# A hybrid decoder layer with 32 experts: the order of the expert tiles and of the weight loads is changed

## What is computed

```python
def hier_moe(h, rg_w, rg_b, re_w, re_b, w_gate, w_up, w_down):
    # top-1 of 4 expert groups, then top-2 of the 8 experts in it: 2 experts for each token
    ...
    def expert_block(args):
        xblk, e = args
        return (jax.nn.silu(xblk @ w_gate[e]) * (xblk @ w_up[e])) @ w_down[e]
    ...
    y = jnp.sum(yb[dest].reshape(T, TOP_K, D) * gate[..., None].astype(h.dtype), axis=1)
```

## Time and profile before

| | |
|---|---|
| median of 3 runs | 1059.0 us (1054.67 to 1060.1) |
| profiled execution | 1059.32 us, its span 1057.6 us |
| TensorE busy (PE) | 960.4 us, 91% |
| VectorE busy (DVE) | 659.9 us, 62% |
| ScalarE busy (ACT) | 459.9 us, 43% |
| moved by DMA | 264.97 MB, 251 GB/s over the span |

### The profile page before, as it was taken

The page is one execution under the profiler, slowest core; times in us unless marked ns, Lnnn a source line. Parts: engine busy times, 40 slices in busy tenths (PEclk is TensorE's granted clock), DMA queues, the critical chain, the costliest instruction groups (busy, mean ns, idle before and its releaser), DMA issues.

```text
span 1057.6 us, 12148 instructions
## 1 busy us (share of the span) xinstructions
PE 960.4 (91%) x4539; PEld 685.7 (65%) x4539; DVE 659.9 (62%) x752; ACT 459.9 (43%) x554; POOL 341.4 (32%) x245
## 2 busy tenths in 40 slices
PE   6999999999999998499999899989986898999981
PEld 5758888887878887375564464455423576888861
DVE  5468999788786677774420431232104587999975
ACT  6576446343662223254220321231104385777762
POOL 0276998932120000202231032022110343423234
PEclk9989999999999999599999999999999989999996
DMA  9520202020072324889799999999999999999774
GB/s 318 173 81 1 80 1 80 0 81 1 5 275 100 120 99 161 312 292 374 271 354 393 414 347 340 417 362 328 420 412 421 410 408 343 356 379 387 263 258 187
DMA packets 65294, 264.97 MB, mean 251 GB/s; under 512 B 10853, under 2 KB 29477, under 8 KB 40656
## 3 DMA queue, kind: packets, MB, share of 16 engines
q1 hardware_dynamic: 51792, 237.07, 57.4%
q0 software_dynamic: 10032, 18.60, 7.1%
q10 hardware_dynamic: 3408, 8.48, 2.1%
HBM read 249.44 MB, written 28.84 MB: 263 GB/s over the span
## 4 chain that ended last, share of the span: by engine, by line
PE 33%; DMA 19%; DVE 5%; ACT 2%; issue 1%; POOL 1%; SPq 0%; POOLq 0%; ACTq 0%; DVEq 0%
PE ps L2260 7%; DMA raw_b<-in_expert_w_down_dram 7%; PE ps L2233 6%; PE ps L2235 6%; PE ps L2234 6%; DMA raw_b<-in_expert_w_up_dram 5%; PE ps L2273 4%; DMA summed_rows<-ym,idx_g 3%; DMA raw<-in_expert_w_up_dram 2%; PE ps L2226 2%; DMA raw<-in_expert_w_down_dram 1%; DVE lo_a L1765 1%; DMA xg<-hf_rows,idx_g 1%; DVE sums L1857 1%; ACT hi_a L1203 1%
## 5 line engine op out<-in xcount | busy, mean ns | idle before, releaser
L2233 PE MATMUL ps<-hi_a,xm_hi 128*128 128x512 f32 x304 | 126.4, 416 | 20.6 <-DVE lo_b L1765 10.3
L824 POOL DMA_INDIRECT summed_rows<-ym,idx_g x25 | 60.8, 2431 | 215.5 <-DVE ym L1814 208.0
L2235 PE MATMUL ps<-hi_a,xm_lo 128*128 128x512 f32 x304 | 124.1, 408 | 0.0
L2260 PE MATMUL ps<-raw,xm 128*64 128x512 f32 x256 | 112.5, 594 | 4.7 <-DMA raw_b<-in_expert_w_up_dram 4.3
L1765 DVE TENSOR_TENSOR lo_a<-raw,hi_a 128x2048 fp32r<-128x2048 f32 x32 | 72.8, 2289 | 65.3 <-ACT hi_a L1203 65.3
L2260 PE MATMUL ps<-raw_b,xm 128*64 128x512 f32 x256 | 112.6, 595 | 0.7 <-DMA raw<-in_expert_w_up_dram 0.7
L1376 DVE SCALAR_TENSOR_TENSOR ps<-uT,pcol,ps 128x1024 f32<-128x1024 f32 (+1 forms) x87 | 96.5, 1109 | 2.4
L735 POOL TENSOR_TENSOR acc<-x,acc 128x1024 f32<-128x1024 f32 x30 | 85.6, 2854 | 31.1 <-ACT x L995 27.0
L1765 DVE TENSOR_TENSOR lo_b<-raw_b,hi_a 128x2048 fp32r<-128x2048 f32 x28 | 63.7, 2291 | 37.7 <-ACT hi_a L1203 37.6
L2233 PEld LDWEIGHTS ps<-hi_a,xm_hi 128*128 128x128 f32 x304 | 59.5, 196 | 39.9 <-DVE lo_b L1765 12.6
L809 POOL DMA_INDIRECT xg<-hf_rows,idx_g x27 | 32.0, 1185 | 160.1 <-PE ps L2226 136.5
(11 more groups left out here) (366 smaller groups left out, 2338.8 us busy)
## 6 DMA issues: line engine op xcount, KB each, us to landing
raw_b<-in_expert_w_gate_dram SPq DMA_DIRECT2D x32, 1024.0 KB, 12.4
raw_b<-in_expert_w_up_dram SPq DMA_DIRECT2D x32, 1024.0 KB, 14.3
raw<-in_expert_w_up_dram SPq DMA_DIRECT2D x32, 1024.0 KB, 14.2
raw<-in_expert_w_gate_dram SPq DMA_DIRECT2D x32, 1024.0 KB, 10.8
raw_b<-in_expert_w_down_dram SPq DMA_DIRECT2D x32, 1024.0 KB, 12.3
raw<-in_expert_w_down_dram SPq DMA_DIRECT2D x32, 1024.0 KB, 11.9
raw<-in_w_in_dram SPq DMA_DIRECT2D x8, 1024.0 KB, 7.1
xa<-in_x_dram SPq DMA_DIRECT2D x8, 512.0 KB, 8.8
```

The source lines that it names most:

```text
L824: return pool.indirect_dma_start(out=sum_dram, out_offset=bass.IndirectOffsetOnAxis(ap=at.bitcast(U32), axis=0), in_=src, in_offset=None, ...
L2233: pe.matmul(dst, x_hi, w_h, start=first, stop=False)
L2235: return pe.matmul(dst, x_lo, w_h, start=False, stop=stop)
L2260: last = pe.matmul(ps[r * BL:(r + 1) * BL, i // 2, :], xm[:, kk, r * BL:(r + 1) * BL], slot(n, i)[:, w], start=(kk == 0), stop=(kk == KC - 1))
```

## The change

Two things. First, `KINDS` is another string with the same counts of each kind. Before, it reads `SS PDEP PDEP PDEP PP` and 11 times S; after, `SSPSPDEPSPDEPDEPSPSSSSSSPSS`. The last two tiles are S in both; the third last is S before and P after. Second, `load_order` comes from a function that runs at build time. It goes through the pieces in the order in which TensorE uses them and gives each a nominal time, and it lets a nominal load queue take 2.9 us for each piece. Whenever that queue is free, it picks, of all pieces whose slot is free by then, the one with the earliest first use.

```diff
-    KINDS = "SS" + "PDEP" * 3 + "PP" + "S" * 11
+    KINDS = "SSPSPDEPSPDEPDEPSPSSSSSSPSS"
...
-        load_order = sorted(((n, i) for n in range(FIXED, NE) for i in range(6)),
-                            key=lambda p: (slot_free(p[0] - 2, p[1])[1], first_use(*p), p))
+        def planned_loads():
+
+            used = sorted(((after_piece(t, i), t, i) for t in range(NS) for i in range(6)))
+            wanted = [(n, i) for n in range(FIXED, NE) for i in range(6)]
+            landed = {(n, i): 0.0 for n in range(FIXED) for i in range(6)}
+            done, queue, plan = [0.0], 0.0, []
+            while wanted:
+                ready, end = len(done) <= len(used), 0.0
+                if ready:
+                    k, t, i = used[len(done) - 1]
+                    ready = all((n, i) in landed for n in tile_pos[t])
+                if ready:
+                    split = 0.0 if KINDS[t] == "P" else T_SPLIT
+                    end = max([done[-1]] + [landed[n, i] + split for n in tile_pos[t]])
+                    end += (T_PAIR if KINDS[t] == "P" else T_ONE) + (T_TURN if i == 3 else 0.0)
+                free = [p for p in wanted if slot_free(p[0] - 2, p[1])[1] < len(done)]
+                now = [p for p in free if done[slot_free(p[0] - 2, p[1])[1]] <= queue]
+                if now and (not ready or queue <= end):
+                    p = min(now, key=lambda p: (first_use(*p), p))
+                    wanted.remove(p)
+                    queue += T_LOAD
+                    landed[p] = queue + T_LAND
+                    plan.append(p)
+                elif ready:
+                    done.append(end)
+                else:
+                    queue = max(queue, min(done[slot_free(p[0] - 2, p[1])[1]] for p in free))
+            return plan
+
+        T_LOAD, T_LAND, T_SPLIT, T_ONE, T_PAIR, T_TURN = 2.9, 2.0, 4.3, 2.85, 3.25, 1.5
+        load_order = planned_loads()
```

## The result

The kernel after the change takes 1047.29 us (median of 7 runs, 1045.44 to 1051.27), the kernel before, beside it on the same chip, 1056.66 us. The ratio is 0.9914, with a 95% interval from 0.9889 to 0.9939: faster by 0.6 to 1.1%. The prediction said 1061, and that a change of more than 0.5% to the faster side had a chance of 0.28. The time is within its range (1044 to 1074), on the side that it thought less likely.

The account below looks back on a forecast made before the run. TensorE was busy 91%, with about 49 us lost between 510 and 891 us, where weight loads set the pace in the fullest stretch. Sum: 1059.3 - 9 + 10 = 1060.3, given as 1061 us; range 1044 to 1074.

Parts of the forecast that it names:

- the stage: From tile 1's first piece to the end of tile 24's down part; a gain of 9 us was forecast before that end.
- Step 1: Spreading the pairs in the tile order: 47 us lost against 49, so hardly anything gained by itself.
- The ledger: DMA against TensorE time per tile: a pair owes 10 us, D with E gives back 16, 11 absorbed per group.
- Step 2: Loads by need instead of slot release: 7.6 us less lost, from 47 to 39.4, rounded to 40.
- The upper bound: Load order: 7.6 us more absorbed in each of three losing groups, lost time falling from 47 to 24 us.
- The hold at place 29: Loads held some 16 us behind a wait for expert place 29's piece 0; no cost while the DMA queue is long.
- the plan's waits starve the DMA queue: Slower rival: 10 us lost at expert place 29, 1071 us; chance 0.14 together with the rival of held scatters.
- Step 3: After tile 24, now a pair: two scatters in sequence instead of one, +10 us, low +7, high +14.
- The rule on the port: DVE with two SBUF inputs contends with GpSimd reading SBUF, the second blocks; both scatters after tile 24 in danger.
- the order is worth what it could be: Faster rival: 24 us stay lost instead of 49, the end costs 8; 1042 to 1050 us; chance 0.28.
- the debt stays: Slower rival: nothing gained before tile 24 and the longer end is paid; 1068 us; chance 0.20.
- The signs: Tile 24's last scatter landing 20 to 22 us after its down projection; TensorE loss near 40 us; wrong if idle under 30.

Follow-up runs that it names:

- tiles_only: Kernel before with the new tile order and the old sort of the loads; 1062.35 us.
- single_and_down: Kernel before; at four places behind a pair, the single expert's gate and up pieces, then the pair's down pieces, go ahead of the later expert's; 1048.99 us.
- single_first: Kernel before; at four places behind a pair, only the single expert's four gate and up pieces go ahead of the later expert's; 1058.3 us.
- nominal_25: Kernel after with the planner's nominal time for a load at 2.5 instead of 2.9 us; 1039.34 us.
- squares_late: Kernel after with ScalarE's first square of the summed rows moved behind the last tile's down splits; 1047.81 us.

## Why the prediction was wrong in its direction

**The sum in parts.** In the profiled executions the stage was to give 9 us and gave 18.2, the tail was to cost 10 and cost 8.0, and 3.7 us came from ahead of both; against the median there is also the base, as the sum starts from an execution of 1059.3 us and the kernel before had a median of 1056.66.

**Step 1, the tile order: nearly right.** The ledger gave 47 us lost instead of 49. Measured by itself (tiles_only) the new tile order loses 36.3 us of idle time and some 15 us by the low clock, together 52 us in the stage. The 47 take 11 us as absorbed also in the first group, where the same paragraph had found 6; with 6 there the ledger gives 52. That spreading the pairs "brings hardly anything by itself" held under the old sort. What the ledger hadn't in it is that the two parts interact: under the plan the same tile order is worth 6 us of the stage, and the tail takes them back. Also, "each stall is followed by a time at the lower clock" isn't so in its own rows: 577.3 to 618.0 us has 8.0 us of idle time at PEclk 1.00. The sum of 10.2 us takes it as 0, rightly.

**Step 2, the load order: this step failed, in its size.** What moves was named, with places and rows. The upper bound, 23 us, held for the change: the stage was 20.3 us shorter than with the old sort in the same tiles (540.9 to 520.6). With 2.5 us it was 26.0 us shorter, beyond that bound. I took a third of it, 7.6 us, "being nearer to the measured margin than to the ideal one". The reason given, that the order "shifts need, it removes no transfer", is where it went wrong. No transfer is removed, but idle time of the queue is: pieces that TensorE needs sooner free their slots sooner, and SP's gaps shrink (single_and_down: 13.3, 14.6 and 15.0 us instead of 20.4, 22.4 and 23.6). The row of that gap was in front of me; I used it as proof that what is given back can't be stored, and took it for fixed. Also, I counted the D tiles' pieces only. The single_first run shows that these by themselves are worth nothing (1058.3 us), the next one that with the pairs' down pieces they are worth 8 us in the old tiles. In the new tiles no run takes the planned order apart like this.

**The hold at place 29: wrong in kind, right in the sum.** It was to last some 16 us and lasted 18.1. It was to cost nothing because issue to landing was 20.9 us. But that latency is the one among pairs; here, behind S tiles, the queue was short and ran dry (49 GB/s). The rival "the plan's waits starve the DMA queue" is thus seen, yet not its 10 us: the other order of the same loads costs as much. Nothing shows that the pair's stall of 5.3 us of idle and 3.5 us of low clock could be had for less by ordering.

**Step 3, the tail: right in kind, 2 to 4 us off.** +10 was forecast, +8.0 measured between the two profiled executions, and about 6 over all of them. The second scatter is issued 7.6 us after the first (8.9 forecast) and lands in 4.6 us (9.2 forecast, the median over all pairs. The last pair holds the smallest experts of its kind, and fewer loads are under way then; no run parts the two). That makes 12.3 us instead of 7.9, +4.3. Another 2.8 us come from ahead of it: the first scatter goes out 6.1 us after the down part instead of 3.3, since VectorE writes `ym` behind two splits of a last tile, and these begin with the end of the down part instead of 2.7 us ahead of it; their tile's pieces land late (ScalarE had waited 8.1 us for one of them, until 978.2 us). This wasn't in the sum. About 1 us of the 8.0 lies behind the last scatter. It landed 18.3 us after the down part, below the 20 to 22 that I gave as the sign.

**The rule on the port.** The prediction named the tail's two scatters as being in danger. The Trainium skill, page "SBUF — State Buffer", section "Who interferes with whom", says that a DVE instruction with two SBUF inputs contends with a GpSimd instruction that reads SBUF, and that the shared ports are an exclusive lock. In one direction the traces agree. While the scatter instruction of 861.50 us before lasted 10.01 us, DVE did this (start us, us, line, op):

```profile
861.12 2.29 DVE L1765 TENSOR_TENSOR lo_a<-raw,hi_a 128x2048 fp32r<-128x2048 f32 x1
863.32 4.50 DVE L1765 TENSOR_TENSOR lo_b<-raw_b,hi_b 128x2048 fp32r<-128x2048 f32 x2
867.73 2.30 DVE L1765 TENSOR_TENSOR lo_b<-raw_b,hi_a 128x2048 fp32r<-128x2048 f32 x1
```

A subtraction of two SBUF operands was already running when the scatter began, three more followed at once, and the scatter ended 1.49 us after the last of them. This is no exception. In the 14 profiled executions such a subtraction was running at the start of 116 scatters, and each of these ended 1.3 to 1.5 us after the end of a subtraction; the other 347 took 1.45 to 1.64 us. In the other direction the traces don't agree. The timelines of POOL and of DVE in the tail after the change:

```profile
990.55 1.45 POOL L853 DMA_INDIRECT summed_rows<-ym,idx_g  x1 [21.18 <-DVE ym L1843]
998.18 1.58 POOL L853 DMA_INDIRECT summed_rows<-ym,idx_h  x1 [6.19 <-DMA summed_rows<-ym,idx_g]
```

```profile
990.71 2.29 DVE L1794 TENSOR_TENSOR lo_a<-raw,hi_a 128x2048 fp32r<-128x2048 f32 x1 [0.45 <-ACT hi_a L1232]
```

The subtraction starts 0.16 us into the scatter instruction and runs 2.29 us; the scatter takes 1.45 us. All 1344 such subtractions of the 14 executions take 2.26 to 2.35 us, also those that begin while a scatter instruction runs (118 scatters had one). So a scatter that comes second waits, and a subtraction that comes second doesn't. Here the tail's two scatters had luck. In three of the six kernels with the pair at tile 24 the second one met a subtraction, took 3.4 to 3.5 us (nominal_25: 990.73 us, 3.36 us) and landed after 6.3 to 6.6 us instead of 4.6.

**The rivals.** The faster one, 0.28, was the right one: "the order is worth what it could be", 24 us lost and 1042 to 1050. Measured were 32 us lost (52 with the old sort in the same tiles) and 1047.3. I argued against it that the DMA share is full from 769.8 to 831.1 and that no order makes room there. That is true of the stretch and beside the point: there was room elsewhere, where the queue ran dry (before, at 515 and 612 us). What speaks for "the debt stays" fell with the run of the load order alone.

**The signs.** Idle time plus low clock was to be near 40 us; it was 32. The bound for being wrong was 30 us of "idle time": idle time alone was 24.9 us, under it, and with the low clock it was just over. The tail from tile 24's end was 59.2 us, above 57. The stalls were to stand before each D tile that follows P S P, around tile 18 and at tile 24 or 25: they did (519 to 565, 626 to 674, 794 to 881, 935 to 984).

## To carry to other kernels

When a queue that waits in order feeds reused buffers, look in the trace for the times at which it is idle, not only at those where it is full: a late consumer frees buffers late, and an order by need can win both times. Check such an order over everything that is needed before the pieces that step back; with one group left behind, the stall only changes its place. Where a planner at build time uses nominal times, set them by the measured rate and try a value on either side: 2.5 instead of 2.9 us was worth 8 us here, nearly as much as the change itself, and 11.5 us in the old tile order, but nothing with the pair at tile 23. So such a value has to be tried again when the tiles move.

## What was not expected of the hardware

- The time until the stage begins is not the same in all executions, though all kernels do the same until then: TensorE's first piece of the mixture was done between 445.9 and 450.9 us, and tile 1's first piece between 461.6 and 468.3 us, in the 14 profiled executions. The later ones have a stretch at the lower clock at about 463 us. So a single profile differs from another by up to 6.7 us for reasons outside the change; stage and tail have to be compared apart.
- A scatter instruction on POOL that starts while DVE subtracts two SBUF operands lasts until a subtraction has ended and 1.3 to 1.5 us more, up to 10.0 us in all; one that starts first takes 1.45 to 1.64 us and doesn't hold DVE.
- The second scatter of the last pair or of half a tile lands in 3.9 to 4.7 us where it isn't held so, 6.3 to 6.6 where it is; the median of the pairs' second scatters was 9.2.
- Eight loads of 512 KB of the summed rows, issued some 0.5 us apart, land one after the other: the first 3.2 us after its issue, the sixth 10.4, the last 11.9 (kernel squares_late; much the same in the kernel after). The first tells little about a chain that needs all of them.
